# 24 tokens instead of 16 take the down product by gathered rows

## What is computed

```
expert[t, 0:128], gate[t, 0:128]     8 heads x 16 experts each, out of 16384
act[t, k] = gelu(w_down[expert[t, k]] . x[t])          (the down product)
out[t]    = sum over k of gate[t, k] * act[t, k] * w_up[expert[t, k]]
x[t]      = layernorm(2**0.25 * x[t] + out[t])
```

## Time and profile before

| | |
|---|---|
| median of 3 runs | 1542.86 us |
| the profiled execution | 1540.33 us, span of its trace 1538.6 us |
| dense down tiles, 128 | 439.8 to 1004.1 us of the span |
| dense up tiles, 128 | 1004.1 to about 1526 us |
| busy PE / DVE / POOL / ACT | 99% / 75% / 49% / 42% |

### The profile page before, as it was taken

One profiled execution on the slowest core, in us unless ns is written; L12 is line 12 of the kernel. 1 busy time (PEld: TensorE's weight loads), 2 busy tenths in 40 slices (PEclk: granted clock), 3 DMA queues, 4 the chain that ended last, 5 costly groups with the idle time before them and its releaser, 6 DMA issues.

```text
span 1538.6 us, 23591 instructions
## 1 busy us (share of the span) xinstructions
PE 1520.6 (99%) x8620; PEld 1369.3 (89%) x8620; DVE 1155.4 (75%) x2400; ACT 639.1 (42%) x852; POOL 755.4 (49%) x469
## 2 busy tenths in 40 slices
PE   8999999999999999999999999999999999999996
PEld 8888899889899999999999999988888888888885
DVE  5564262477999979777878785888888888888796
ACT  5323244423234456536743663443333333333333
POOL 1543481324345887878786878532222223222230
PEclk9999999999999999999999999999999999999999
DMA  8532250333246999999999999989999999999981
GB/s 303 199 97 95 84 182 23 123 110 111 82 134 191 334 321 319 336 416 379 299 357 415 363 323 359 369 331 338 354 352 338 352 338 346 354 341 356 369 324 55
DMA packets 145821, 418.24 MB, mean 272 GB/s; under 512 B 17952, under 2 KB 52016, under 8 KB 145200
## 3 DMA queue, kind: packets, MB, share of 16 engines
q1 hardware_dynamic: 100216, 252.84, 47.2%
q0 software_dynamic: 39168, 142.62, 24.8%
q10 hardware_dynamic: 6328, 21.33, 3.5%
HBM read 371.36 MB, written 45.37 MB: 271 GB/s over the span
## 4 chain that ended last, share of the span: by engine, by line
PE 93%; DMA 4%; POOL 1%; DVE 1%; ACT 0%; issue 0%; SPq 0%; DVEq 0%; ACTq 0%
PE ps L1749 11%; PE ps L1751 11%; PE ps L1750 11%; PE ps L1318 10%; PE ps L1319 9%; PE ps L1320 9%; PE ps L433 6%; PE ps L434 6%; PE ps L435 6%; DMA act_d<-act_t 3%; PE ps L1702 1%; PE ps L1173 1%; PE ps L1174 1%; PE ps L1175 1%; PE ps L1704 1%; PE ps L1184 1%
## 5 line engine op out<-in xcount | busy, mean ns | idle before, releaser
L1581 ACT ACTIVATE w_hi<-raw 128x1024 fp32r<-128x1024 f32 x252 | 266.6, 1058 | 339.2 <-PE ps L1751 300.5
L1318 PE MATMUL ps<-b_hi,w_hi 128*128 128x368 f32 x1024 | 341.2, 333 | 1.5 <-ACT act_t L1587 1.3
L1319 PE MATMUL ps<-b_lo,w_hi 128*128 128x368 f32 x1024 | 336.5, 329 | 0.0
L1320 PE MATMUL ps<-b_hi,w_lo 128*128 128x368 f32 x1024 | 336.3, 328 | 0.0
L1542 POOL TENSOR_TENSOR w_lo<-raw,w_hi 128x1024 fp32r<-128x1024 f32 x119 | 287.0, 2413 | 73.6 <-ACT w_hi L1581 72.0
L1555 POOL DMA_INDIRECT rows<-in_w_up,expert x128 | 149.9, 1171 | 344.4 <-DVE ps L1870 329.8
L1750 PE MATMUL ps<-w_lo,b_hi 128*128 128x512 f32 x768 | 298.8, 389 | 0.0
L1749 PE MATMUL ps<-w_hi,b_hi 128*128 128x512 f32 x768 | 298.8, 389 | 0.0
L1751 PE MATMUL ps<-w_hi,b_lo 128*128 128x512 f32 x768 | 298.8, 389 | 0.0
L1791 DVE SCALAR_TENSOR_TENSOR rows<-rows,ps 128x1024 f32<-128x1024 f32 x144 | 174.4, 1219 | 80.2 <-DMA rows<-in_w_down,expert 64.8
L1877 DVE TENSOR_TENSOR w_lo<-raw,w_hi 128x1024 fp32r<-128x1024 f32 x133 | 162.8, 1224 | 71.1 <-ACT w_hi L1581 71.0
(11 more groups left out here) (288 smaller groups left out, 2507.4 us busy)
## 6 DMA issues: line engine op xcount, KB each, us to landing
raw<-in_down_t SPq DMA_DIRECT2D x128, 512.0 KB
raw<-in_up_t SPq DMA_DIRECT2D x128, 512.0 KB
raw<-in_units SPq DMA_DIRECT2D x75, 512.0 KB, 3.4
act_d<-act_t SPq DMA_DIRECT2D x124, 192.0 KB
c<-act_d SPq DMA_DIRECT2D x124, 192.0 KB
gate_d<-gmat ACTq DMA_DIRECT2D x32, 512.0 KB
v<-gate_d SPq DMA_DIRECT2D x16, 512.0 KB
i<-gate_d SPq DMA_DIRECT2D x16, 512.0 KB
```

Of the source, the lines that this page charges most:

```text
L1318: nc.tensor.matmul(out, ring.w_hi[:, s, w], b_hi[:, c, 0:T], start=c == 0, stop=False)
L1319: nc.tensor.matmul(out, ring.w_hi[:, s, w], b_lo[:, c, 0:T], start=False, stop=False)
L1320: last = nc.tensor.matmul(out, ring.w_lo[:, s, w], b_hi[:, c, 0:T], start=False, stop=c == KC - 1)
L1581: nc.scalar.activation(w_hi[:, u % W4, :], raw[:, u % W4, :], ACT.Copy).then_inc(hi_done, 1)
```

## The change

XT becomes 24. It follows that T = 360, XQ = 5 (groups of 24 tokens, 120 rows in a gather), XM = 26, NR = 154. The first extra row is X_FIRST = 106. A block of 33 tiles makes 43 dots in place of 41 (one more in each of two gate rounds), and tiles 110 to 127 make 25 in place of 21. Block 2 has 13 common rounds and 3 extra ones in place of 14 and 2. The constants of the tail move: ACT's wait (DOT_TILE) is in step 111 and for dot 131; the coefficients are loaded by SP in step 114 and made in step 116; the extra rounds stand after tiles 118, 120 and 122; the first products of the up pass are made in step 124.

In the list of steps, gather 106 (the first extra one) stands in POOL's step 96, behind no other, and gathers 131 to 134 in step 111, where before 125 to 128 stand.

```diff
-XT = 16
+XT = 24
 T = DT - XT
 XQ = P // XT
-XM = HK // XQ
+XM = -(-HK // XQ)
+XP = XQ * XT
 XS = P - XT
 XROUNDS = XT // RT
 NR = HK + XM
-ASK_TILE, DOT_TILE, COEF_TILE = 93, 110, 115
-X_ROUND_TILES = (118, 121)
-PRODUCT_TILE = 123
+ASK_TILE, DOT_TILE, COEF_TILE = 93, 111, 116
+X_ROUND_TILES = (118, 120, 122)
+PRODUCT_TILE = 124
...
-BLOCK_DOTS = tuple(range(1, 18)) + (17,) + tuple(i for i in range(18, 33) for _ in range(1 + (i % 2 or i == 32)))
-X_FIRST = 2 * len(BLOCK_DOTS) + 22
+BLOCK_DOTS = tuple(range(1, 18)) + (17,) + tuple(i for i in range(18, 33) for _ in range(1 + (i % 2 or i in (22, 28, 32))))
+X_FIRST = 2 * len(BLOCK_DOTS) + 20
...
-                    sp.dma_start(t["x_ids_d"], k["flat"][XS:].rearrange("p h k -> p (h k)")).then_inc(x_ids_stored, 16)
+                    ids = k["flat"][XS:].rearrange("p h k -> p (h k)")
+                    sp.dma_start(t["x_ids_d"][:, 0:HK], ids).then_inc(x_ids_stored, 16)
+                    sp.dma_start(t["x_ids_d"][:, HK:], ids[:, 0:XQ * XM - HK]).then_inc(x_ids_stored, 16)
                 if u == ASK_TILE + 1:
-                    sp.wait_ge(x_ids_stored, 16)
+                    sp.wait_ge(x_ids_stored, 32)
...
-                    sp.dma_start(x_coef[:, 0], t["x_act_d"].rearrange("t k -> k t"),
+                    sp.dma_start(x_coef[:, 0], t["x_act_d"][:, 0:HK].rearrange("t k -> k t"),
...
-                nc.gpsimd.indirect_dma_start(rows[:, j, :], None, t["w_down"] if r < NR else t["w_up"],
+                nc.gpsimd.indirect_dma_start(rows[0:P if x is None else XP, j, :], None, t["w_down"] if r < NR else t["w_up"],
...
-                if u == PRODUCT_TILE + 2:
+                if u == PRODUCT_TILE + 1:
                     h_high(0)
...
-                row, x = rows[:, j, :].rearrange("p (i c) -> p i c", i=2), extra_row(r)
+                x = extra_row(r)
+                n = P if x is None else XP
+                row = rows[0:n, j, :].rearrange("p (i c) -> p i c", i=2)
...
-                nc.vector.scalar_tensor_tensor(out=row, in0=row, scalar=1.0, in1=xb, op0=ALU.mult, op1=ALU.mult,
+                nc.vector.scalar_tensor_tensor(out=row, in0=row, scalar=1.0, in1=xb[0:n], op0=ALU.mult, op1=ALU.mult,
...
-                    dots_until(made[0] + (4 if i == 1 else 1 + i % 2))
+                    dots_until(made[0] + (4 if i == 1 else 1 + (i % 2 or i in (4, 10))))
...
-                if u == X_ROUND_TILES[0] + 1:
-                    extra_ready(1)
+                if u - 1 in X_ROUND_TILES[:-1]:
+                    extra_ready(X_ROUND_TILES.index(u - 1) + 1)
...
-                if u == PRODUCT_TILE + 4:
+                if u == PRODUCT_TILE + 3:
                     low(0)
```

More of the change, by code:

```diff
@@ L1390, in program @@
         coef = gparts[:, 0].rearrange("p h k -> p (h k)")
-        x_expert, x_dots, x_coef = sb("x_expert", [P, XM], U32), sb("x_dots", [P, XM]), sb("x_coef", [P, 2, XT])
+        x_expert, x_dots, x_coef = sb("x_expert", [XP, XM], U32), sb("x_dots", [XP, XM]), sb("x_coef", [P, 2, XT])
         x_part = sb("x_part", [P, 3, XT], BF16)
@@ L1787, in dot @@
                     dve.wait_ge(row_free, r)
-                    step(nc.vector.tensor_copy(xb.rearrange("p i (c j) -> p (i c) j", j=P), xb_in if x is None else x_rows))
+                    step(nc.vector.tensor_copy(xb[0:n].rearrange("p i (c j) -> p (i c) j", j=P),
+                                               xb_in[0:n] if x is None else x_rows[0:n]))
                     done()
                 into = dn[:, gathered_row(r):gathered_row(r) + 1] if x is None else x_dots[:, x:x + 1]
-                nc.vector.scalar_tensor_tensor(out=row, in0=row, scalar=1.0, in1=xb, op0=ALU.mult, op1=ALU.mult,
+                nc.vector.scalar_tensor_tensor(out=row, in0=row, scalar=1.0, in1=xb[0:n], op0=ALU.mult, op1=ALU.mult,
                                                accum_out=into).then_inc(row_free, 1)
@@ L2043, in build @@
         t["act_d"] = nc.dram_tensor("act_d", (TILES, P, DT), F32, kind="Internal").ap()
-        t["x_ids_d"] = nc.dram_tensor("x_ids_d", (XT, HK), U32, kind="Internal").ap()
-        t["x_act_d"] = nc.dram_tensor("x_act_d", (XT, HK), F32, kind="Internal").ap()
+        t["x_ids_d"] = nc.dram_tensor("x_ids_d", (XT, XQ * XM), U32, kind="Internal").ap()
+        t["x_act_d"] = nc.dram_tensor("x_act_d", (XT, XQ * XM), F32, kind="Internal").ap()
         t["gate_d"] = nc.dram_tensor("gate_d", (KEPT, P, TILES * P), F32, kind="Internal").ap()
```

## The result

The kernel after takes **1570.54 us** (median of 4 runs, 1567.05 to 1571.79) against 1543.05 for the kernel before (4 runs beside it, 1541.06 to 1544.13): ratio **1.0175, 95% interval 1.0163 to 1.0187**, so 27 us slower. The forecast was 1544.1 with a range up to 1550.0, and it is wrong. The profiled execution took 1571.79 us, its span 1570.0, 31.4 longer than the span of before.

What follows compares the result with a forecast made beforehand. PE, busy 99% of the span, was taken to bound the kernel, held to the DMA's pace in the choice tiles. Terms -10.2 + 0.5 + 2.6 + 0.3 + 3.5 + 4.3 + 0.3 = +1.3 us gave 1544.1 us, range 1536.5 to 1550.

Steps and rivals of the forecast that it cites:

- as sums they cost nothing: Ten more gathers and dots fit DVE's 385 us free and the rounds' 100 GB/s of DMA room; only their place counts.
- The columns: Dense tiles: 8 columns fewer at 0.417 ns each, a straight line, save 3.33 ns in each of 3072 matmuls, -10.2 us.
- small rival on columns: Dense matmuls: columns worth less than the straight line, -3.2 us in place of -10.2, total 1549.4 us; chance 0.05.
- The choice tiles: Blocks 1 and 2: DMA sets where some 16 tiles end, losing 1.3 us of gain in each block, +2.6 us (0 to 2.8).
- ACT's wait for the last extra dot: Step 111, dot 131: gather and dot end late, so PE waits before tile 114, +3.5 us (2.4 to 4.6).
- The load of the coefficients: SP's load, one tile less before tile 118 and 3072 elements, delays the first extra round, +4.3 us (0 to 7).
- Rounds two tiles apart: Between extra rounds DVE needs 8.6 us, PE takes 9.3, so it fits: +0.3 us (0 to 2 x 2.3).
- Block 2's rounds near the first extra gather: Block 2's rounds: first extra gather 1 us later and one more dot, against a 1.6 us lead, +0.3 us (0 to 1.5).
- The waits of the tail don't reach PE: Tail of block 2: only rounds and choice tiles take from the gain, 1535.8 us; chance 0.27 with one-wait-gone cases.
- The extra rounds bind: Extra rounds: bf16 products take 5.14 us each time instead of 2.14, delaying rounds, 1549.9 us; chance 0.25.

Runs made afterwards that it cites:

- e4: The kernel before with 360 dense columns instead of 368, the product of the cut columns left out: 1539.72 us, ratio 0.9988.
- e13: e12 with ACT's wait back at tile 110, coefficients at 115 and SP's load at 113, first extra round still at 118: 1542.99 us, ratio 1.0007.
- e12: e1 with 16 extra gathers and dots in place of 26, placed in the tiles as in the kernel before: 1545.87 us, ratio 1.0026.
- e1: The changed kernel with 128 rows instead of 120 in each of its 26 extra gathers: 1551.10 us, ratio 1.0063.
- e9: e1 with its 26 extra gathers fetching 64 rows each, all dots kept: 1552.82 us, ratio 1.0072.
- e5: e1 with coefficients made in step 118 and extra rounds after tiles 120, 122 and 124: 1549.45 us, ratio 1.0049.

## Why the prediction was wrong

With the ratios set in a row, each run one step from the next, and 0.1% being 1.54 us:

| from | to | ratio | us |
|---|---|---|---|
| before | 360 columns (e4) | 0.9988 | -1.9 |
| e4 | third round, its loads and stores (e13) | 1.0007 | +2.9 |
| e13 | ACT's wait, the load and the coefficients one tile later (e12) | 1.0026 | +2.9 |
| e12 | ten more gathers and dots of 128 rows (e1) | 1.0063 | +5.7 |
| e1 | 120 rows in place of 128 (after) | 1.0175 | +17.3 |

Sum +27. The intervals of the last four (0.9997 to 1.0016, 1.0017 to 1.0036, 1.0046 to 1.0080, 1.0163 to 1.0187) don't touch, so each step behind e13 is shown. The first two are less sure: the interval of e4 ends where that of e13 begins, and each leaves 1.5 us either way.

**The step that failed: "as sums they cost nothing".** The ten gathers and dots were priced at their instructions and their bytes, 26 x 120 rows as 4.4 MB more. The price of a gather of 120 rows was none of my terms. Every gather of the kernel before has 128 rows, so no row of its trace could show one of 120, and I bounded the rest of my unknown costs but not this one. It is the largest, 17.3 us, and it alone puts the time out of the range. The two terms that it broke are the +0.3 for the rounds of block 2 and the +3.5 for ACT's wait, whose 6.8 us until the dot came from a gather of 128 rows.

**The same step again, at 128 rows: 5.7 us.** I looked for room in sums (DVE 385 us free, 100 GB/s to spare), not at the order. e9 shows that the bytes weren't it, e12 that without the ten ACT has no wait at all. What is left is that they stand in POOL's and DVE's queues; that POOL's issues are the tighter of the two is argued, not shown, and the time that each gather takes to land is not excluded (e9). The order of the steps says where it bites. Before, the gather of the last extra dot is in POOL's step 107, the dot in DVE's step 108, and ACT waits for it in step 110. With the ten more, gather, dot and wait are all in step 111: three steps later for the dot, one for the wait. No run gave the extra gathers earlier places.

**The columns.** -10.2 us forecast, -7.0 by the starts (164.4 ns, not 163.3): eight columns gave 2.3 ns and not 3.33. The direction of the small rival on columns was right, its size wasn't. The figure of the Trainium skill ("TensorE: Matmul & The Clock Gate", section "Back-to-back issue gap") gives 1.0 ns for eight columns and -3.2 us; the measured step lies between it and the straight line, nearer to the line, and some tiles have the 160.0 ns that would be better than either.

**The choice tiles.** Right in kind: from the start of tile 44 to that of 61, 69.6 us before and 70.1 after; from 77 to 94, 70.0 and 70.3. None of the gain is kept: 2 x 17 x 24 x 0.0023 = 1.9 us of it, where 2.6 was forecast from a gain of 3.33 ns. The 0.5 and 0.3 more are within the spread of the runs (69.3 to 71.0 and 69.0 to 70.7 in the nine with 360 columns; their means are 70.2 and 69.9, those of the five with 368 are 69.9 and 70.0). What I missed is a wait in block 0, where I had written that it keeps its gain: 2.4 us at tiles 14 and 15, by POOL's wait for the experts, and 1.3 at the round in tile 34.

**ACT's wait for the last extra dot.** The wait stands where it was forecast, at tile 114. With 128 rows it is 5.0 us and 1.5 more of restart, against 3.5 (2.4 to 4.6). Dot 131 was made at 947.7, from a gather issued at 939.04: 8.7 us from issue to the end of the dot, where I had 8.0; the rest is that it was issued 5.9 us after the end of tile 110 (933.2), not 5.4, and the restart, for which there was no term. In the changed kernel the gather was issued 10.9 us after the start of tile 111 (945.58), and the dot began 10.3 us behind the issue (956.51 to 966.76) in place of 6.8; the wait is 11.1 and its restart 1.7. (The sum of that term comes to 15.4, not 15.3, which changes nothing.)

**The load of the coefficients.** Forecast +4.3, measured 4.6 with 128 rows and 4.0 in the changed kernel. The size is right. In e1 the chain from the issue (958.55) to the end of the products (974.26) took 15.7 us, inside the 13.5 to 16.5 of the forecast, but its parts are others than those that I had counted on in the middle. I had the load scaled with its elements, 8.9 us (half of 7.0 scaled by a half gives 8.75); it took 7.5 in e1 and 7.0 in the changed kernel. Over all runs it is 6.7 to 9.3 with 2048 elements and 7.0 to 9.4 with 3072, so no scaling shows. The products were the long ones, held by POOL's split. And DVE can come to the coefficients late from dots that wait for gathers, for which I had nothing. Moving the steps a tile nearer to the round costs 2.9 us of the tile's 3.95 (e12 against e13).

**Rounds two tiles apart.** Right: in e1 and in the changed kernel no wait of PE above 0.4 us stands before the second or third extra round.

**Block 2's rounds near the first extra gather.** Forecast 0.3 (0 to 1.5). In e1 it is 0.6, at tile 100. In the changed kernel it is 4.1 and 0.9 there and 2.2 and 1.6 at tile 106, the gathers again.

**The rivals.** "The waits of the tail don't reach PE" had 0.27 and is refuted in each run that has all 26 gathers. "The extra rounds bind" named a real mechanism, the long products, but gave them to every round; the traces show them where POOL splits. That the time would rise had 0.30 in all, but no rival named a rise of 27 us, nor the shape of the gathers as its cause.

No version here that computes everything beats the kernel before: the nearest is e5, at 1.0049.

## What to carry to other kernels

When a change alters the shape of a DMA, not only its number, treat its price as unknown until a run of that shape has been seen: the cheapest repair here was to fetch more (128 rows in place of 120, 17 to 19 us). Time that one engine saves has to be followed to the next wait on every other engine whose work didn't shrink; of 7.0 us saved by PE, 2.6 were left. And a queue with free time on average is not free where a deadline stands: take out the added instructions in one run and the added bytes in another before blaming either.

## What the runs showed of the hardware

**Gathers of a number of rows that 16 doesn't divide** (120, 104): 144 packets whichever, and 251 to 256 ns for 4 KB, against 176 at 128 rows and 215 and 225 at 112 and 64. Weight loads of 512 KB beside them landed after 10.7 us (120) and 7.8 (104), beside gathers of 64, 112 and 128 rows after 5.1, 5.7 and 6.8 (the last in e1). **Short gathers are not cheap ones**: 64 rows landed in 5.2 us, 128 in 6.2.

**A product of DVE in bf16 and a split of POOL exclude each other.** Three products of 0.68 us take 1.90. Each product of over 0.75 us in five traces (before, after, e1, e12, e13) lies across a split: in the kernel before 961.64 to 964.94 with a split at 961.97 to 964.38, in e13 962.35 to 965.76 with one at 962.81 to 965.20. It ends 0.55 us after the split has. e5's nine have no split beside them, and all take 0.69. It is always the product that is held, also where it has begun first, as in these two; no such split takes more than 2.42 us. The Trainium skill states it ("SBUF — State Buffer", section "Who interferes with whom"): DVE and GpSimd share one pair of ports, an exclusive lock. The trace agrees; this is the 5.14 us that I had taken from the earlier trace rows without asking where they came from.

**A wait of PE costs again behind it.** The windows of the kernel after behind the wait before tile 111 (columns as above):

```profile
943.70:945.40 1.70, 0.08 (x1) 0.00 (x0) 0.00 (x0) 0.43 (x1) 0.00 (x0) 1.00 1.06 276
945.60:946.80 1.20, 1.20 (x7) 1.20 (x8) 0.15 (x1) 0.00 (x0) 0.00 (x0) 0.97 1.02 280
946.90:949.90 3.00, 3.00 (x12) 3.00 (x11) 1.86 (x3) 1.33 (x2) 1.33 (x1) 0.50 1.04 290
950.00:953.00 3.00, 3.00 (x20) 3.00 (x19) 0.53 (x3) 0.30 (x2) 2.52 (x3) 0.98 1.02 320
```

PE stood for 1.8 us; it resumes at 2.4 GHz, is granted 1.2 GHz (0.50) for 3 us with starts 300 ns apart, and is back. That made tile 111 1.6 us longer, almost as much as the wait itself. In the changed kernel such restarts are 0.9, 1.6, 1.6 and 1.7 us behind the waits at tiles 100, 106, 110 and 113: 5.8 us for which the prediction had no term.
